# Expert steps of two 64-row lanes, three token lists gathered directly, and unit-matrix turnings in TensorE's waits, in a two-layer hybrid trunk with a mixture of experts

## The reference

```python
def hier_moe(h, rg_w, rg_b, re_w, re_b, w_gate, w_up, w_down):
    ...
    g_p, g_i = lax.top_k(g_prob, 1)
    e_prob = jax.nn.softmax(e_logits[rows, g_i[:, 0]], axis=-1)
    e_p, e_i = lax.top_k(e_prob, TOP_K_IN_GROUP)
    w = g_p * e_p / jnp.sum(e_p, axis=-1, keepdims=True)
    ids = g_i * EXPERTS_PER_GROUP + e_i
    combine = jnp.zeros((T, N_EXPERTS), F32).at[rows[:, None], ids].add(w)
    hid = jax.nn.silu(jnp.einsum('td,edf->tef', t, w_gate)) * jnp.einsum('td,edf->tef', t, w_up)
    y = jnp.einsum('tef,efd->td', hid * combine[:, :, None], w_down)
```

## Time and profile before

| | us |
|---|---|
| median of 3 runs (2176.8 to 2179.28) | 2176.97 |
| the profiled execution | 2177.04 |
| its span, first to last instruction | 2175.2 |
| PE busy in the span | 2034.2 |
| DVE, ACT, POOL busy | 948.7, 492.6, 128.0 |
| granted TensorE clock, mean share | 0.969 |

### The profile page before, as it was taken

The page is one execution under the profiler, slowest core; times in us unless marked ns, Lnnn a source line. Parts: engine busy times, 40 slices in busy tenths (PEclk is TensorE's granted clock), DMA queues, the critical chain, the costliest instruction groups (busy, mean ns, idle before and its releaser), DMA issues.

```text
span 2175.2 us, 23007 instructions
## 1 busy us (share of the span) xinstructions
PE 2034.2 (94%) x9027; PEld 1376.8 (63%) x9027; DVE 948.7 (44%) x1998; ACT 492.6 (23%) x791; POOL 128.0 (6%) x193
## 2 busy tenths in 40 slices
PE   5999999999999997999589999999999999799993
PEld 2787776667777783444258777666776668544441
DVE  1135028667756863111252531476676128511115
ACT  1241113434410011111134310134344000111112
POOL 2000000000000002000210000000000000200001
PEclk9999999999999998999889999999999999799997
DMA  9661112333264337999661111142323430699974
GB/s 358 227 228 47 31 47 80 124 102 103 69 213 145 136 116 296 360 354 362 251 189 58 60 36 39 32 134 88 117 83 113 145 106 40 227 346 364 353 295 164
DMA packets 172698, 360.93 MB, mean 166 GB/s; under 512 B 11536, under 2 KB 124816, under 8 KB 161648
## 3 DMA queue, kind: packets, MB, share of 16 engines
q1 hardware_dynamic: 145808, 269.43, 35.8%
q0 software_dynamic: 19408, 64.70, 8.2%
q10 hardware_dynamic: 7376, 25.33, 2.9%
HBM read 303.52 MB, written 58.52 MB: 166 GB/s over the span
## 4 chain that ended last, share of the span: by engine, by line
PE 80%; DMA 10%; DVE 5%; issue 1%; ACT 1%; POOL 1%; SPq 1%; ACTq 0%; DVEq 0%; POOLq 0%
PE PS L979 75%; DMA ring<-in_expert_w_up_dram 6%; PE PS L983 4%; DMA ar<-in_ada_w_dram 1%; DVE ar L1576 1%; POOL rows L955 1%; DMA mg<-rows 1%; DMA xr<-out_y_dram 1%; DMA br<-rows,posi 1%; DVE xr L535 1%; PE PS L682 1%; DMA rows<-br,posi 1%; ACT hT L1374 0%; SPq L813 0%; DVE br L1576 0%
## 5 line engine op out<-in xcount | busy, mean ns | idle before, releaser
L979 PE MATMUL PS<-hT,ring 128*128 128x320 f32 (+1 forms) x2624 | 719.5, 439 | 5.8 <-DVE hT L672 4.2
L979 PEld LDWEIGHTS PS<-hT,ring 128*128 128x128 f32 (+1 forms) x2624 | 486.6, 189 | 214.9 <-issue 11.2
L979 PE MATMUL PS<-ring,mg 128*128 128x512 f32 (+1 forms) x1552 | 554.2, 512 | 25.0 <-DMA ring<-in_expert_w_up_dram 11.6
L979 PEld LDWEIGHTS PS<-ring,mg 128*128 128x128 f32 x1552 | 291.3, 192 | 234.7 <-issue 205.1
L535 DVE SCALAR_TENSOR_TENSOR xr<-ring,cs,xr 128x256 f32<-128x256 f32 x560 | 246.7, 482 | 9.9
L979 PE MATMUL PS<-br,ring 128*128 128x320 f32 x768 | 215.6, 434 | 0.8 <-DVE br L1773 0.8
L979 PEld LDWEIGHTS PS<-br,ring 128*128 128x128 f32 x768 | 145.1, 190 | 64.2 <-issue 4.2
L1576 DVE TENSOR_TENSOR mg<-PS,mg 128x256 f32<-128x256 f32 x38 | 16.1, 424 | 380.5 <-ACT mg L1374 380.5
L1374 ACT ACTIVATE xr<-PS 128x256 f32<-128x256 f32 (+1 forms) x108 | 56.0, 524 | 553.7 <-PE PS L979 553.6
L979 PE MATMUL PS<-ring,hT 128*128 128x256 f32 x800 | 177.4, 381 | 1.7 <-DVE ar L1576 1.7
L979 PEld LDWEIGHTS PS<-ring,hT 128*128 128x128 f32 x800 | 150.5, 190 | 26.2 <-issue 5.6
(11 more groups left out here) (229 smaller groups left out, 1465.6 us busy)
## 6 DMA issues: line engine op xcount, KB each, us to landing
ring<-in_w_in_dram SPq DMA_DIRECT2D x50, 1024.0 KB, 7.9
ring<-in_ada_w_dram SPq DMA_DIRECT2D x40, 1024.0 KB, 5.2
ring<-in_expert_w_gate_dram SPq DMA_DIRECT2D x38, 1024.0 KB, 8.5
ring<-in_expert_w_up_dram SPq DMA_DIRECT2D x38, 1024.0 KB, 10.6
ring<-in_expert_w_down_dram SPq DMA_DIRECT2D x38, 1024.0 KB, 5.3
rows<-br ACTq DMA_DIRECT2D x38, 512.0 KB, 8.9
mg<-rows SPq DMA_DIRECT2D x36, 512.0 KB, 11.4
rows<-const POOLq DMA_DIRECT2D x1, 13824.0 KB, 55.1
```

The lines of the kernel that those rows point to most:

```text
L979: return nc.tensor.matmul(out, lhsT, rhs, start=start, stop=stop, skip_group_check=True)
```

## The change

Steps take the place of tiles. Step s (0 to 15) holds 64 rows of expert s, its own lane, and 64 rows of a guest, an expert that has more than 64 rows and whose weights are still in SBUF. The weights of four experts are kept (`HOMES`), in one buffer `store` that joins what were `ring`, `hT` and `br`. The guest's place is a number that PE reads from `exi` in each step, and its matmuls take their address from that register. Both lanes are computed by matmuls with 64 stationary columns into the two halves of the PSUM partitions. Step 0 holds 128 rows of expert 0. Rows that find no lane go to 128-row tiles: step 16 always runs, more in the loop, whose range grows to 8 skipped iterations (`TILES` 34). Three steps (`DIRECT` 3) get their tokens by list: list 0 as before, lists 1 and 2 from the places, between PE's products of step 0. DVE has more arithmetic for the places. PE turns the unit matrix (`kept_running`) in eight kinds of places. The zero fill of `rows` grows from 27 to 35 tiles of 512 KB and is split in two.

```diff
+HOMES, HOME = 4, 3 * BLK
+LANE = P // 2
...
+        def kept_running(ps, n):
+            for _ in range(n):
+                nc.tensor.transpose(ps[:, 0:P], ident, ident)
...
         def experts_summed(pe, was, on, t):
+            ps = on.wait_slot(pe, ("sum", t))
+            if t == 1:
+                pe.wait_ge(was.experts_done, 1)
+                kept_running(ps, 56)
+                pe.wait_ge(was.first_in[1], 16 * 2)
+                kept_running(ps, 16)
             pe.wait_ge(was.yg_in[t - 1], 16 * 2)
-            ps = on.wait_slot(pe, ("sum", t))
...
+                for e in range(2, NE):
                     on.wait_filled(sp, ("gu", e - 2))
                     for part in range(2):
-                        strip_load(e, e % 2, part)
+                        strip_load(e, e % 2, part, e % HOMES)
+                    if e == 2:
+                        sp.wait_ge(on.scattered, 16 * 2 * T)
                     on.wait_filled(sp, ("xg", e - 1))
                     rows_load(e + 1, (e + 1) % 2)
                     on.wait_filled(sp, ("dn", e - 2))
-                    down_load(e, e % 2)
+                    down_load(e, e % 2, e % HOMES)
...
+                pool.wait_ge(on.route_ready, FIRST_LISTED)
+                listed_rows(0)
                 pool.wait_ge(on.route_ready, PLACES)
                 for t in range(T):
+                    if 1 <= t < DIRECT:
+                        pool.wait_ge(on.route_ready, PLACES + t)
+                        if t == 2:
+                            on.wait_filled(pool, ("xg", 0))
+                        listed_rows(t)
                     for w in range(2):
                         pool.indirect_dma_start(rows, ...)
...
                             ps = on.wait_slot(pe, key)
+                            if h == 0 and t >= 3:
+                                kept_running(ps, 10)
                             pe.wait_ge(on.x_norm, t + 1)
...
+                kept_running(on.wait_slot(pe, ("lr",)), 10 if l else 24)
...
+                ps = on.wait_slot(pe, ("rank",))
+                kept_running(ps, 22)
                 pe.wait_ge(on.masks_ready, 1)
...
+                def lanes_gate_up(s):
+                    ...
+                    own = strips(slice(HOME * (s % HOMES), HOME * (s % HOMES) + 2 * BLK))
+                    guest = strips(bass.ds(guests[s], 2 * BLK)) if s else None
+                    for k in range(KD):
+                        if s == 0 and k in (3, 5):
+                            listed(k // 2)
+                        if s == 0:
+                            last = mm(out, xgT[0][:, k, :], own[:, k, :, :], k == 0, k == KD - 1)
+                        else:
+                            mm(out[0:LANE], xgT[s % 2][:, k, 0:LANE], guest[:, k, :, :], k == 0, k == KD - 1)
+                            last = mm(out[LANE:P], xgT[s % 2][:, k, LANE:P], own[:, k, :, :], k == 0, k == KD - 1)
+                def lanes_down(s):
+                    ...
+                                mm(ps[0:LANE, cols], hidT[s % 2][:, f, 0:LANE], guest[:, f, cols], f == 0, f == 1)
+                                last = mm(ps[LANE:P, cols], hidT[s % 2][:, f, LANE:P], own[:, f, cols], f == 0, f == 1)
...
+                kept_running(on.wait_slot(pe, ("xg", 0)), 27)
+                rows_here(0, 0)
                 rows_turned(0, 0)
-                for j in range(NE):
+                for j in range(NE + 1):
+                    if j == 1:
+                        pe.wait_ge(on.route_ready, LANES)
+                    if 1 <= j < NE:
+                        guests[j] = pe.value_load(exi[0:1, j:j + 1], min_val=0, max_val=HOME * (HOMES - 1))
                     on.wait_slot(pe, ("gu", j))
+                    if j == 0:
+                        kept_running(on.slot(("gu", 0)), 6)
...
                 pairs = pe.value_load(exi[0:1, TILES:TILES + 1], min_val=NE // 2, max_val=TILES // 2 - 1)
-                with pe.Fori(NE // 2, TILES // 2) as i:
+                with pe.Fori(NE // 2, TILES // 2 - 1) as i:
...
-                gate_up(2, pairs - 1)
-                rows_turned(3, pairs - 1)
-                down(1, pairs - 1)
-                hidden_turned(2, pairs - 1)
                 down(2, pairs - 1)
```

More of the change, by code:

```diff
@@ new lines, in _ @@
+                listed(0)
+                on.wait_moved(dve, ("rank",))
+                halves, over, lane, first, held, left, end, back, jump = (
+                    R[n] for n in ("halves", "over", "lane", "first", "held", "left", "end", "back", "jump"))
+                cmp9, cmp5 = (R["cmp"][:, 0:n * NE].rearrange("p (e j) -> p e j", e=NE) for n in (9, 5))
+                ramp = slot[:, 0:NE]
+                step(V.tensor_scalar(halves, R["rk"][:, NE * T:NE * (T + 1)], 1.0 / LANE, None, ALU.mult))
@@ new lines, in _ @@
+                step(tt(cmp9, bc(halves.unsqueeze(2), [P, NE, 9]), bc(slot[:, 0:9].unsqueeze(1), [P, NE, 9]), ALU.is_gt))
+                step(V.tensor_reduce(over, cmp9, AXL.X, ALU.add))
+                step(V.tensor_tensor_scan(lane, ramp, over, 0.0, ALU.max, ALU.add))
+                step(tt(first, lane, over, ALU.subtract))
+                step(V.scalar_tensor_tensor(out=held, in0=slot[:, HOMES - 1:HOMES - 1 + NE], scalar=NE + 1.0, in1=first, op0=ALU.min, op1=ALU.subtract))
+                step(V.scalar_tensor_tensor(out=held, in0=held, scalar=0.0, in1=over, op0=ALU.max, op1=ALU.min))
@@ new lines, in _ @@
+                step(tt(left, halves, held, ALU.subtract))
+                step(tt(cmp5, bc(left.unsqueeze(2), [P, NE, 5]), bc(slot[:, 0:9:2].unsqueeze(1), [P, NE, 5]), ALU.is_gt))
+                step(V.tensor_reduce(left, cmp5, AXL.X, ALU.add))
+                step(V.tensor_tensor_scan(end, cst("ones")[:, 0:NE], left, float(NE), ALU.mult, ALU.add))
+                step(tt(back, end, left, ALU.subtract))
+                step(V.scalar_tensor_tensor(out=back, in0=held, scalar=-0.5, in1=back, op0=ALU.mult, op1=ALU.add))
@@ new lines, in _, with per_token, by_token @@
+                step(tt(jump, first, ramp, ALU.subtract))
+                step(V.tensor_scalar(jump, jump, float(P), -float(P), ALU.mult, ALU.add))
+                def per_token(row):
+                    return bc(row.unsqueeze(1), [P, T, NE])
+                def by_token(name):
+                    return R[name][:, 0:T * NE].rearrange("p (t e) -> p t e", t=T)
+                rk3, at3, el3, eq3, run3 = (by_token(n) for n in ("rk", "at", "el", "eq", "run"))
+                step(V.scalar_tensor_tensor(out=at3, in0=rk3, scalar=float(LANE), in1=per_token(jump), op0=ALU.is_ge, op1=ALU.mult))
```

283 lines of the change are left out of this document (164 added, 119 removed).

## The result

The changed kernel takes 2144.43 us (median of 4 runs, 2142.63 to 2147.15), before 2176.89 (2173.59 to 2179.28): the ratio is 0.9853, 95% interval 0.9841 to 0.9865, a gain of 32 us. The forecast was 2119, in a range of 2104 to 2137: the direction was right, the gain a little over half of what was forecast, and the time lies 7 us above the range. The profiled execution of the change took 2145.14 us with a span of 2143.3, so its rows can be laid beside those of before (span 2175.2).

The account below looks back on a forecast made before the run. It took PE, busy 94% of the span, as the limit, nearly balanced with weight transfers in the experts. Gains of 46 (experts), 4 (entry) and 7.9 us (clock), 57.9 in all, off 2177.04 gave 2119 us, range 2104 to 2137.

Parts of the forecast that it names:

- Fewer tiles: Expert loop: both layers have 17 steps instead of 19 tiles, two fewer each, seen as 34 issues of a matrix.
- lanes side by side: Expert steps: two 64-column matmuls in different column halves run together, 32 passes in some 7 us.
- registers: Guest addresses in each step: load and register changes hidden by the sequencer's lead, 0 us, at most 1 to 2 a step.
- loop's end: After step 16: eight skipped iterations put the last down 8.8 us after the end of gate and up.
- rival of lanes in turn: Expert steps: register addresses make the lanes run one after another, 10.4 us more a step, 2430 us; chance 0.04.
- exposed addresses: Lane steps: register work not hidden, 1.2 to 2.5 us a step, 2155 to 2194 us; chance 0.04.
- A step's price: Lane step: 11.9 us, between 11.74 and 12.3, with four changes of shape at 0.39 us together.
- The end of the experts: Last down: lost cover costs 2.1 us a layer, waits of 2.85 and 2.53 go; with fewer steps, gain 46 us.
- The entry: Start of the experts: first gate and up at full clock, minus two lists inside; 2 us a layer, 4 together.
- rows of step 3 come late: Rival at the experts' entry: rows of step 3 late, costing 6 us a layer, 2131 us; chance 0.14.
- The turnings: Sums, both `lr` and other waits: unit-matrix turnings hold PE's full clock, gaining 7.9 us.
- The rival by the Trainium skill: Waits filled with turnings: transposes don't hold the clock, so the 7.9 us vanish, 2127 us; chance 0.14.

Follow-up runs that it names:

- weights_ahead: Changed kernel with SP issuing gate and up of the next expert ahead of down of the present one: 2135.62 us, 0.9817.
- all_three: Changed kernel with LayerNorm loads held back, one branch around the loop over further tiles, and gate and up ahead of down on SP: 2119.12 us, 0.9739.
- whole_steps: Changed kernel with products by 128-column matmuls from the step's own weights, no lanes or registers, guest rows multiplied with wrong weights: 2129.07 us, 0.9790.
- loop_guard: Changed kernel with one branch around the whole loop over further tiles, on PE, DVE, ACT and SP: 2133.51 us, 0.9805.
- fixed_guest: Changed kernel with guest weights from the step's own fixed place, no number load or register work, wrong weights for guest rows: 2138.38 us, 0.9835.
- turn_step3: Changed kernel with 40 more unit-matrix turnings in PE's wait for the rows of step 3: 2141.99 us, 0.9839.
- rows_first: Changed kernel with SP waiting until the rows of step 3 landed before issuing down of expert 2 and gate and up of expert 3: 2147.82 us, 0.9859.
- ln_later: Changed kernel with POOL's four LayerNorm broadcast loads issued after gate and up of step 16, not right behind the scatters: 2138.21 us, 0.9825.

## Why the prediction was wrong

The forecast's direction and most of its mechanisms held; three terms of its sum were mis-sized, by 27 us together, and the clock outside the experts brought 1 us more than its term.

- **Fewer tiles, lanes side by side, registers, loop's end: right.** 34 issues; 32 passes in 7.02 us; a fixed address changes nothing in the step; the last down starts 8.4 us after the gate and up, where 8.8 stood. The rival of lanes in turn and that of exposed addresses are out.
- **A step's price, 7 us short.** The 11.96 us without waits came out (11.99), partly by luck: a whole step without a wait takes 11.46 us, not 11.57, and the four changes of shape cost 0.53 us, not 0.39. Wrong was the choice of 11.9 "because PE without a wait (11.57 + 0.39 = 11.96) then meets a transfer-bound 11.74": I took the two limits as if the slower one hid the other. The steps took 12.22 and 12.11 us, 13 x 0.32 + 13 x 0.21 = 6.9 us more. Of these 2.3 us are PE's own 11.99, and 4.6 are waits for weights, which did not vanish with a slower PE, since they came from SP's order and not from volume: `weights_ahead` shows 11.99 once the order is mended. Whether the transfers' volume bound the tile of 11.74 in the kernel before stays open: its view showed 358 GB/s, `all_three` moves as much without a wait in layer 0, and `whole_steps`, in the old order, still had waits at 359.
- **The end of the experts, 3.5 us short.** The wait was forecast, its effect on the clock was not. Behind gaps of 3.40 and 3.16 us the last down took 5.39 and 6.59 us instead of 3.70 (4.6 us together, less 0.4 and 0.7 for a start that came sooner than forecast). `loop_guard` shortens the gap to 1.64 us, and the slow passes go. The length of the gap does not fix that price: in `fixed_guest` the last down of layer 0 took 3.70 us behind a gap of 3.44.
- **The entry, the largest, 16 us short.** From first to fourth gate and up the layers lost 6.7 and 5.7 us, where a gain of 2 each was forecast. "It is tight" was the right reading and 2 us a layer the wrong sum. Its timing of the rows was nearly right: the scatters ended at 853.06 (852 forecast), the rows came at 862.8 (861.4). But PE was through with step 2's gate and up at 856.8, not at "about 860.5": the first list's gather went out at 817.31 and not still at 820.35, and the first gate and up began 3.7 us sooner. I had counted such gains, and the full clock of the first gate and up, as if they came through: a wait that ends at a fixed time swallows what is gained ahead of it. And the sum timed the rows only. It named the weights of step 3 behind the same wait on SP and gave them no time; up landed at 870.6, so step 3 could not begin before that even with the clock held behind the rows' wait (`turn_step3`). The rival "rows of step 3 come late" named the place and its price (6 us a layer); it was given 0.14. What it lacked was the cause: POOL's four LayerNorm loads, which I never costed since they stand in both programs. Beside them the row load took 9.4 us in the kernel before as well, where PE waited 2.37 us for it; I carried the 9.4 over without asking what made it.
- **The turnings: right.** 7.9 us were forecast, and 7.9 is what they bring in the kernel before (interval 5.7 to 11.5 us); in the changed kernel the four stretches outside the experts gained 8.8 us, and without the turnings they are 9.4 longer. The eight first passes of a sum take 3.54 us (3.44 forecast), `lr` of layer 1 starts its 32 first passes within 4.07 us. The rival by the Trainium skill, "TensorE: Matmul & The Clock Gate", Part 4, that transposes don't count as work for the clock, is contradicted: 40 of them hold it in `turn_step3`, and leaving all out costs 0.8%.

That `all_three` lands on the 2119 us of the forecast is chance as much as confirmation: it has three edits that the forecast did not have.

## What to carry to other kernels

A gain ahead of a wait that ends at a fixed time is worth nothing: before adding terms, ask for each stage which transfer ends last there, and list every transfer in flight at that time, those that the change leaves alone included. An in-order issue queue can make two streams wait for each other's events; if one load stands behind another that is allowed only later, reading the queue's own timeline shows it, and here the swap of a few lines was worth 9 us. And a wait on TensorE can have two prices, its length and the slow products behind it: both were paid at the last down, the second not at step 3 of the changed kernel, where the weights came as late.

## What the hardware showed beyond that

- Two 64-column products in different halves start 6 to 13 ns apart in most pairs of the changed kernel and take one product's time (32 passes in 7.02 us, 16 full ones in 6.94), with one address from a register; a change between 128 and 64 columns costs 0.13 us on average (11.99 - 11.46 us over four).
- A row load of 512 KB took 9.1 us beside four broadcast loads of as many bytes each on another queue (`rows_first`), with none of its own queue's transfers beside it. Without the broadcast loads it took 3.5 us, though 3 MB of weights were issued right behind it on its own queue (`ln_later`).
- The granted clock was 0.61 in 862.8 to 870.8 us, right behind a gap of 6.04 us, though PE was busy before it; behind 40 unit-matrix turnings in that gap it stayed at 1.00, and the same down took 3.65 instead of 5.75 us.
